# Two transformer blocks in one kernel: four layer seams run by token tile, x loaded in four transfers, the feed-forward of TensorE without its loop

## What is computed

```python
proj = x @ w_in[l]                      # 2048 -> 7168 columns
mix = concat(conv_mixer(...), hgrn2_mixer(...), retention_mixer(...))
x = layer_norm(ALPHA * x + mix @ w_out[l], ln1_g[l], ln1_b[l])
f = square(relu(x @ w_ff1[l]))          # 2048 -> 8192
x = layer_norm(ALPHA * x + f @ w_ff2[l], ln2_g[l], ln2_b[l])
```

## Time and profile before

| | |
|---|---|
| median of three runs | 3609.84 us |
| the profiled execution | 3611.74 us, its span 3609.9 us |
| mean granted TensorE clock | 0.981 |
| busy share of the span | TensorE 96%, VectorE 60%, ScalarE 45%, GpSimd 9% |
| chain that ended last | TensorE 85%, VectorE 8%, ScalarE 3%, DMA 2%, GpSimd 1%, issue 1% |
| moved by DMA | 617 MB, 171 GB/s over the span |

### The profile page before, as it was taken

One profiled execution on the slowest core, in us unless ns is written; L12 is line 12 of the kernel. 1 busy time (PEld: TensorE's weight loads), 2 busy tenths in 40 slices (PEclk: granted clock), 3 DMA queues, 4 the chain that ended last, 5 costly groups with the idle time before them and its releaser, 6 DMA issues.

```text
span 3609.9 us, 43760 instructions
## 1 busy us (share of the span) xinstructions
PE 3458.3 (96%) x16363; PEld 2890.7 (80%) x16363; DVE 2178.5 (60%) x2436; ACT 1618.2 (45%) x1953; POOL 329.4 (9%) x220
## 2 busy tenths in 40 slices
PE   7999999999999999999999999999999978999999
PEld 6888778888878787877888888888888777788877
DVE  5986565555555688865655555566456643656654
ACT  4544434444434346434444344444446533355553
POOL 0025000000000000330100000000000141000100
PEclk9999999999999999999999999999999989999999
DMA  6645555656555565446656565656656400565635
GB/s 211 189 139 158 180 182 186 192 186 187 186 185 185 171 194 156 146 146 204 220 189 187 192 187 191 188 185 206 184 173 178 143 6 14 185 191 174 177 121 163
DMA packets 311336, 617.02 MB, mean 171 GB/s; under 512 B 19305, under 2 KB 19305, under 8 KB 309243
## 3 DMA queue, kind: packets, MB, share of 16 engines
q1 hardware_dynamic: 306144, 591.73, 53.0%
q0 software_dynamic: 5024, 22.88, 1.9%
HBM read 612.44 MB, written 2.10 MB: 170 GB/s over the span
## 4 chain that ended last, share of the span: by engine, by line
PE 85%; DVE 8%; ACT 3%; DMA 2%; POOL 1%; issue 1%; SPq 0%; DVEq 0%; ACTq 0%; POOLq 0%
PE ps_unit L247 26%; PE ps_unit L249 26%; PE ps_unit L248 25%; DVE sb_w_lo L232 2%; PE ps_mix L2287 2%; DVE sb_conv_y L865 2%; PE ps_mix L939 1%; PE ps_mix L371 1%; PE ps_mix L525 1%; ACT sb_w_hi L225 1%; DMA sb_raw<-in_w_in_dram 1%; PE ps_mix L2285 0%; DMA sb_raw<-in_w_ff_dram 0%; DMA sb_raw<-in_e_w_in_dram 0%; PE ps_mix L2642 0%
## 5 line engine op out<-in xcount | busy, mean ns | idle before, releaser
L232 DVE TENSOR_TENSOR sb_w_lo<-sb_raw,sb_w_hi 128x1024 fp32r<-128x1024 f32 x1120 | 1407.6, 1269 | 1048.4 <-ACT sb_w_hi L225 1043.3
L225 ACT ACTIVATE sb_w_hi<-sb_raw 128x1024 fp32r<-128x1024 f32 x1120 | 1178.6, 1060 | 1483.4 <-DMA sb_raw<-in_w_ff_dram 740.9
L247 PE MATMUL ps_unit<-sb_w_hi,sb_a_hi 128*128 128x512 f32 x3456 | 1366.8, 395 | 26.7 <-DVE sb_a_lo L411 18.3
L249 PE MATMUL ps_unit<-sb_w_hi,sb_a_lo 128*128 128x512 f32 x3456 | 1351.7, 391 | 0.0
L248 PE MATMUL ps_unit<-sb_w_lo,sb_a_hi 128*128 128x512 f32 x3456 | 1351.3, 391 | 0.0
L247 PEld LDWEIGHTS ps_unit<-sb_w_hi,sb_a_hi 128*128 128x128 f32 x3456 | 653.6, 189 | 162.2 <-DVE sb_a_lo L411 19.8
L249 PEld LDWEIGHTS ps_unit<-sb_w_hi,sb_a_lo 128*128 128x128 f32 x3456 | 652.7, 189 | 138.2
L248 PEld LDWEIGHTS ps_unit<-sb_w_lo,sb_a_hi 128*128 128x128 f32 x3456 | 653.8, 189 | 132.3
L247 PE MATMUL ps_unit<-sb_w_hi,sb_f_hi 128*128 128x512 f32 x1024 | 400.0, 391 | 0.0
L249 PE MATMUL ps_unit<-sb_w_hi,sb_f_lo 128*128 128x512 f32 x1024 | 398.7, 389 | 0.0
L248 PE MATMUL ps_unit<-sb_w_lo,sb_f_hi 128*128 128x512 f32 x1024 | 398.4, 389 | 0.0
(11 more groups left out here) (447 smaller groups left out, 1986.1 us busy)
## 6 DMA issues: line engine op xcount, KB each, us to landing
sb_raw<-in_w_ff_dram SPq DMA_DIRECT2D x512, 512.0 KB, 3.7
sb_raw<-in_w_in_dram SPq DMA_DIRECT2D x224, 512.0 KB, 3.6
sb_raw<-in_e_w_in_dram SPq DMA_DIRECT2D x112, 512.0 KB, 3.5
sb_raw<-in_o_w_in_dram SPq DMA_DIRECT2D x112, 512.0 KB, 3.6
sb_raw<-in_w_out_dram SPq DMA_DIRECT2D x64, 512.0 KB, 4.5
sb_raw<-in_e_w_out_dram SPq DMA_DIRECT2D x32, 512.0 KB, 4.6
sb_raw<-in_o_w_out_dram SPq DMA_DIRECT2D x32, 512.0 KB, 3.8
sb_raw<-in_e_w_mem_kv_dram SPq DMA_DIRECT2D x16, 512.0 KB, 3.7
```

The lines of the kernel that those rows point to most:

```text
L225: k.nc.scalar.activation(k.w_hi[:, j], k.raw[:, j], ACT.Copy).then_inc(k.hi_ready, 1)
L232: k.nc.vector.tensor_tensor(k.w_lo[:, j], k.raw[:, j], k.w_hi[:, j].bitcast(F32), ALU.subtract).then_inc(k.lo_ready, 1)
L247: k.nc.tensor.matmul(acc, hi[:, kt, tokens], w_hi, start=kt == 0, stop=False)
L249: last = k.nc.tensor.matmul(acc, lo[:, kt, tokens], w_hi, start=False, stop=kt == KT - 1)
```

## The change

- At the four seams the last unit (`pe_seam_last`) runs blocks 0 to 3 for both tiles, then blocks 4 to 7 for tile 0, then blocks 4 to 7 for tile 1. The first unit behind the seam (`pe_seam_first`) runs blocks 0 to 3 for tile 0, then for tile 1, then 4 to 7 for both.
- A bank of a seam holds 512 channels of one tile (`SEAM_BANKS`). Residual, statistics and aggregate of tile 0 wait for `tile_done`, those of tile 1 for the unit. The norm is done for the first 1024 channels by tile, then for 512 channels of both tiles at a time, with the splits of blocks 3, 4 and 5 of the next unit between (`dve_seam`; `act_seam` on ScalarE).
- ALPHA is folded into the residual add of the out-projections; for the feed-forward GpSimd scales x behind the last bank of the seam (`pool_scale_residual`), and VectorE waits for that before its first residual there.
- At the start x comes in four transfers of 512 channels, each ahead of two blocks of weights, and splits and banks alternate on ScalarE and VectorE.
- On TensorE the groups of the feed-forward and the units of these out-projections are written out instead of looped.

The diff, cut:

```diff
+def sp_first_units(sp, k, x, weights):
+    w = weights.rearrange("(kt p) n -> p kt n", p=P)
+    for c in range(CONV_UNITS * BLOCKS):
+        j, at = c % BLOCKS, c // BLOCKS * NC
+        if c % 2 == 0 and c // 2 < D // NC:
+            cols = slice(c // 2 * NC, (c // 2 + 1) * NC)
+            sp.dma_start(k.x[:, :, cols], tokens(x)[:, :, cols]).then_inc(*k.x_in[c // 2].up(16))
+        sp.wait_ge(k.block_done, c + 1)
+        sp.dma_start(k.raw[:, j], w[:, KB * j:KB * (j + 1), at:at + NC]).then_inc(k.raw_ready[j], 16)
+    k.block0["sp"] += CONV_UNITS * BLOCKS
...
-def pe_block(pe, k, b0, c, hi, lo):
+def pe_block(pe, k, b0, c, hi, lo, tiles=range(TT)):
     s, j = c // BLOCKS % 2, c % BLOCKS
-    if j == 0:
-        pe.wait_ge(k.evacuated, b0 + (c + BLOCKS))
-    pe.wait_ge(k.lo_ready, b0 + (c + 1))
+    if 0 in tiles:
+        if j == 0:
+            pe.wait_ge(k.evacuated, b0 + (c + BLOCKS))
+        pe.wait_ge(k.lo_ready, b0 + (c + 1))
     for n in range(KB):
         kt = KB * j + n
-        for t in range(TT):
+        for t in tiles:
             tokens = slice(t * P, (t + 1) * P)
             acc = k.ps_unit[:, s, t, :]
             w_hi, w_lo = k.w_hi[:, j, n, :], k.w_lo[:, j, n, :]
             k.nc.tensor.matmul(acc, hi[:, kt, tokens], w_hi, start=kt == 0, stop=False)
             k.nc.tensor.matmul(acc, hi[:, kt, tokens], w_lo, start=False, stop=False)
             last = k.nc.tensor.matmul(acc, lo[:, kt, tokens], w_hi, start=False, stop=kt == KT - 1)
-    last.then_inc(k.block_done, 1)
+    if TT - 1 in tiles:
+        last.then_inc(k.block_done, 1)
+    return last
...
+SEAM = BLOCKS // 2
+SEAM_BANKS = ((0, 0), (0, 1), (1, 0), (1, 1), (0, 2), (1, 2), (0, 3), (1, 3))
...
+def pe_seam_bank(pe, k, tile, n):
+    t, c = SEAM_BANKS[n]
+    pe.wait_ge(*k.turn_source.next("pe"))
+    if n >= 4:
+        pe.wait_ge(*k.turn_lo.next("pe bank"))
+    for x in range(4):
+        last = k.nc.tensor.transpose(k.ps[:, n % 4, x * P:(x + 1) * P], tile(4 * c + x, t), k.ident)
+    last.then_inc(*k.turned.up())
+def pe_seam_last(pe, k, b0, u, hi, lo, tile):
+    c0 = u * BLOCKS
+    for j in range(SEAM):
+        pe_block(pe, k, b0, c0 + j, hi, lo)
+    for j in range(SEAM, BLOCKS):
+        last = pe_block(pe, k, b0, c0 + j, hi, lo, (0,))
+    last.then_inc(*k.tile_done.up())
+    for j in range(SEAM, BLOCKS):
+        pe_block(pe, k, b0, c0 + j, hi, lo, (1,))
+        if j == BLOCKS - 2:
+            pe_seam_bank(pe, k, tile, 0)
+    pe_seam_bank(pe, k, tile, 1)
+def pe_seam_first(pe, k, b0, tile):
+    for t in range(TT):
+        for j in range(SEAM):
+            if j % 2 == 0:
+                pe.wait_ge(*k.turn_lo.next("pe"))
+            pe_block(pe, k, b0, j, k.a_hi, k.a_lo, (t,))
+            if (t, j) in ((0, 2), (0, 3), (1, 1), (1, 2)):
+                pe_seam_bank(pe, k, tile, {(0, 2): 2, (0, 3): 3, (1, 1): 4, (1, 2): 5}[t, j])
+    for j in range(SEAM, BLOCKS):
+        if j % 2 == 0:
+            pe.wait_ge(*k.turn_lo.next("pe", TT))
+        pe_block(pe, k, b0, j, k.a_hi, k.a_lo)
+        if j == SEAM:
+            for n in (6, 7):
+                pe_seam_bank(pe, k, tile, n)
+    k.turn_lo.next("pe bank", 4)
...
+def act_seam(act, k, b0, c0, root):
+    act_sqrt_table(k)
+    act_split(act, k, b0, c0 + SEAM - 1)
+    for t in range(TT):
+        root(t)
+        for n in (2 * t, 2 * t + 1):
+            act_seam_bank(act, k, n)
+    for c in (SEAM, SEAM + 1):
+        act_split(act, k, b0, c0 + c)
+    for n in range(4, 8):
+        act_seam_bank(act, k, n)
...
+def dve_seam(dve, k, b0, u, chunk, norm):
+    c0 = (u + 1) * BLOCKS
+    def statistics(t):
+        cols = slice(chunk * NC, (chunk + 1) * NC)
+        x = k.x[:, t, cols]
+        if t == 0:
+            dve.wait_ge(*k.tile_done.next("dve"))
+        else:
+            wait_unit(dve, k, b0, u)
+        ins = add_residual(k, x, k.ps_unit[:, u % 2, t], norm.scale)
+        if t == 0:
+            ins.then_inc(*k.dve_step.up())
+            dve.wait_ge(*k.dve_step.now())
+        else:
+            ins.then_inc(k.evacuated, BLOCKS)
+            dve.wait_ge(k.evacuated, b0 + (u + 3) * BLOCKS)
+        ins = k.nc.vector.bn_stats(k.stats[:, t, chunk, :], x)
+        if t == 0:
+            ins.then_inc(*k.dve_step.up())
+            dve.wait_ge(k.stats_ready, k.stats_units - 1)
+            dve.wait_ge(*k.dve_step.now())
+        else:
+            ins.then_inc(k.stats_ready, 1)
+            dve.wait_ge(k.stats_ready, k.stats_units)
+        norm.aggregate(dve, k, t)
+    statistics(0)
+    norm.columns(dve, k, 0, (0, 1))
+    dve_seam_bank(dve, k, 0)
+    statistics(1)
+    dve_seam_bank(dve, k, 1)
+    dve_split(dve, k, b0, c0 + SEAM - 1)
+    norm.columns(dve, k, 1, (0, 1))
+    dve_seam_bank(dve, k, 2)
+    dve_seam_bank(dve, k, 3)
+    for c in (2, 3):
+        norm.columns(dve, k, None, (c,))
+        dve_split(dve, k, b0, c0 + SEAM + c - 2)
+        for t in range(TT):
+            dve_seam_bank(dve, k, 2 * c + t)
+class LayerNorm:
+    def __init__(self, scale):
+        self.scale = scale
+    def aggregate(self, dve, k, t):
+        k.nc.vector.bn_aggr(k.mv[:, t, :], k.stats[:, t].rearrange("p c s -> p (c s)")).then_inc(*k.aggregated.up())
+    def columns(self, dve, k, tile, chunks):
+        v = k.nc.vector
+        tiles = range(TT) if tile is None else (tile,)
+        if tile == 0:
+            dve.wait_ge(*k.row_in.next("dve", 32))
+        dve.wait_ge(*k.aggregated.now())
+        parts = [(t, slice(c * NC, (c + 1) * NC)) for c in chunks for t in tiles]
+        for t, cols in parts:
+            last = v.scalar_tensor_tensor(k.x[:, t, cols], k.x[:, t, cols], k.mv[:, t, 0:1], k.gain[:, cols],
+                                          ALU.subtract, ALU.mult)
+        last.then_inc(*k.dve_step.up())
+        if tile is not None:
+            dve.wait_ge(*k.root.next("dve"))
...
+class RootMeanSquare:
...
+        v = k.nc.vector
+        tiles = range(TT) if tile is None else (tile,)
+        if tile is not None:
+            if tile == 0:
+                dve.wait_ge(*k.row_in.next("dve", 16))
+            dve.wait_ge(*k.rms_root.next("dve"))
+            v.reciprocal(k.ss[:, tile, 1:2], k.ss[:, tile, 1:2]).then_inc(*k.dve_step.up())
+            dve.wait_ge(*k.dve_step.now())
+        for c in chunks:
+            cols = slice(c * NC, (c + 1) * NC)
+            for t in tiles:
+                v.scalar_tensor_tensor(k.normed_x[:, t, cols], k.x[:, t, cols], k.ss[:, t, 1:2], k.gain[:, cols],
+                                       ALU.mult, ALU.mult).then_inc(*k.turn_source.up())
...
+def dve_out_units(dve, k, norm):
+    first = k.block0["dve"]
+    k.block0["dve"] += OUT_UNITS * BLOCKS
+    k.stats_units += OUT_UNITS
+    for u in range(OUT_UNITS - 1):
+        for c in range(AHEAD, AHEAD + BLOCKS):
+            if c == AHEAD + BLOCKS - 1:
+                residual(dve, k, first, u, u, norm.scale)
+            dve_split(dve, k, first, u * BLOCKS + c)
+    last = OUT_UNITS - 1
+    for c in range(AHEAD, BLOCKS + SEAM - 1):
+        dve_split(dve, k, first, last * BLOCKS + c)
+    dve_seam(dve, k, first, last, last, norm)
 def pe_units(pe, k, units, tile=None):
...
+def residual(dve, k, b0, u, chunk, scale=None):
     wait_unit(dve, k, b0, u)
     cols = bass.ds(chunk * NC, NC)
-    k.nc.vector.tensor_tensor(k.x[:, :, cols], k.x[:, :, cols], k.ps_unit[:, u % 2],
-                              ALU.add).then_inc(k.evacuated, BLOCKS)
+    add_residual(k, k.x[:, :, cols], k.ps_unit[:, u % 2], scale).then_inc(k.evacuated, BLOCKS)
...
-def dve_scale_residual(dve, k):
-    dve.wait_ge(*k.turn_lo.now())
-    k.nc.vector.tensor_scalar(k.x[:], k.x[:], ALPHA, None, ALU.mult).then_inc(*k.dve_step.up())
-    dve.wait_ge(*k.dve_step.now())
...
+def pool_scale_residual(pool, k):
+    k.nc.gpsimd.tensor_scalar(k.x[:], k.x[:], ALPHA, None, ALU.mult).then_inc(*k.x_scaled.up())
...
+                pe_seam_first(pe, k, b0, tile)
+                continue
+            if after and g0 == FF_GROUPS - 1 and u == FF_UNITS - 1:
+                pe_seam_last(pe, k, b0, u, hi, lo, after)
+                continue
             for j in range(BLOCKS):
                 if u == 4 and j == 0:
...
-    def turn_step(u, j):
-        if u == 0:
-            pe_turn_step(pe, k, tile, j)
-    pe_turn_start(pe, k, tile)
-    group(0, 0, turn_step)
-    with pe.Fori(0, FF_GROUPS - (2 if between else 1)) as q:
-        group(q, 1)
-    if between:
-        group(0, FF_GROUPS - 1, between)
+    group(0, 0)
+    for q in range(1, FF_GROUPS):
+        group(0, q, between if q == FF_GROUPS - 1 else None)
 def turned_unit(k, u):
     return k.ps[:, 2 * (u % 2):2 * (u % 2) + 2, :].rearrange("p b (a s) -> p (b a) s", a=2)
...
+            if norm and u == FF_UNITS - 1:
+                dve_split(dve, k, b0, u * BLOCKS + AHEAD + 4)
+                dve_seam(dve, k, b0, u, u - 4, norm)
+                continue
             for j in range(AHEAD + 4, AHEAD + 8):
```

(49 more changed lines are left out.)

117 lines of the change are left out of this document (87 added, 30 removed).

## The result

The kernel after the change takes **3580.3 us** (median of six runs, 3578.3 to 3581.6), beside 3616.7 us (3609.0 to 3619.8, six runs) of the kernel before on the same chip. The ratio is **0.9908**, 95% interval 0.9898 to 0.9919: faster by 0.9%. Forecast were 3563.6 us and a range of 3552 to 3580, so the change is faster, as forecast, but by 0.92% where 1.28% were forecast, and the time lies just above the range. (The six executions before spread over 11 us, so the quotient of the two medians, 0.9899, is not quite the ratio.) The profiled execution took 3581.3 us for a span of 3579.5: 30.4 us less span than before, where the sum had 46.2.

A forecast was written before the change was run, and what follows sets the result against it. TensorE, busy 96% of the span, was taken as the bound. Seams 12.4, 8.1 and 7.4, start 10.0, loop 6.6 and ReLU 1.7 sum to 46.2 us saved, giving 3563.6 us against the median; range 3552 to 3580.

The forecast's parts named there:

- the part on ALPHA: Two seams before a feed-forward: GpSimd's scale takes 3.7 us (or 7.6), costing TensorE 2.0 us more in each.
- rival (1): GpSimd's scale runs at the product's rate, 7.6 us; split 3.9 later, clock drops: time 3574, chance 0.10.
- The mechanism of the hold: Seams before a feed-forward: VectorE's split of block 6 is held until GpSimd's scale ends; TensorE waits 2.0 us.
- The walk of the seam: Step-by-step count of a norm seam after the change: waits 4.8 plus eight banks 2.8, 7.6 us instead of 15.9.
- Seam 2: Seam into layer 1, without a scale: cost falls from 15.7 to 7.6 us, a gain of 8.1.
- The start: Kernel start, x in quarters: first matmul at 14.3 instead of 24.27 us, -10.0 us, bounds 8 and 11.5.
- The loop: Layer 0's feed-forward back edges: unlooped code loses the waits on "issue" and low clock, -6.6 us, bounds 4.7 and 7.2.
- the ReLU: Layer 1's squared ReLU: TensorE's single 1.7 us wait disappears, -1.7 us, bounds 0 and 1.9.
- (2): Low clock enters the seams: three norm seams lose 1.5 to 3 us each, time 3568 to 3573, chance 0.14.
- (3): VectorE needs 0.1 to 0.2 us more at each of 25 seam steps, 3 us per seam: 3575, chance 0.06.
- (4): Straight code stalls for fetches like the loop and x's quarters arrive no earlier: time 3577, chance 0.05.
- (5): Slower: TensorE stays at the low clock through each seam, time about 3690, chance 0.02.

The follow-up runs named there:

- e5: Changed kernel with GpSimd's scale replaced by a copy of x onto itself, ALPHA left out of that residual: 3573.3 us, one run.
- e1: Changed kernel without GpSimd's scale, ALPHA folded into the residual adds of the first feed-forward group: 3560.4 us, ratio 0.9855.
- e9: e1 with five GpSimd instructions (scales, a copy, a product) on an unused tile ahead of everything: 3563.8 us, one run.
- e11: e1 with GpSimd's first seven small transfers waiting for the second quarter of x: 3558.4 us, ratio 0.9852.
- e6: Changed kernel with GpSimd's scale replaced by the product x * x of the same 4096 elements: 3572.8 us, one run.
- e2: Changed kernel with the scale on VectorE again, one pass behind the last bank: 3569.7 us, ratio 0.9888.
- e7: Kernel before with the new start alone (x in four transfers, splits and banks in turn): 3603.7 us, ratio 0.9978.

## Why the prediction was wrong, and where it was right

**The step that failed** is one term of the part on ALPHA: "I take 3.7, since scale and copy both read one tensor". The number of inputs does not set GpSimd's time. Measured for 4096 elements: copy 3.61, product 7.01, scale 10.56 us. The choice between the two bounds of the earlier trace rows was argued by likeness, and both bounds were taken for ends although neither row is a scale. The upper one was 3 us too low.

**A second term of the same step** was put at nothing: the clock behind the hold. The forecast charges 2.0 us for the wait and no low clock, and rival (1) prices the clock only for a wait of nearly 6. With e5's copy, which takes the forecast's 3.7 us, the wait is the forecast's 2.0, and 1.5 us of low clock come on top in each seam: -5.1 and -4.9 where -6.2 was forecast. So with the right length too the two seams would have given some 2.4 us less than the sum has.

**The range** ended 0.3 us short of the time. Its upper end also rests on a slip: two of the rivals together, at the prices that the text gives (10.4, up to 9, and 12), come to 3583 to 3586, not 3580. The bounds named for its lower end come to 3553.5, not 3552.

**The mechanism of the hold was right.** A split behind the scale is held, it is the split of block 6, and TensorE waits for it: forecast 2.0, measured 7.1. The forecast's rule (the held split ends 1.1 us behind GpSimd) would with 10.56 us have given 8.9. Behind the wait come 2.4 us of low clock. 7.3 and 2.4, less 2.0, are 7.7; the table has 7.4, and most of the difference is that the rest of the seam costs 7.4 and not 7.6.

**The walk of the seam held in its sum, and partly by luck.** Forecast 7.6 us instead of 15.9. With the scale away (e1) the seam is 8.5 cheaper, 7.4. Read by pitches, as the forecast did, the waits of e1's first seam come to 3.6 us where 4.8 were forecast, the longest 1.4 where mine was 2.2 (the list of waits has 1.2, since it leaves out what the pipeline takes to refill). A bank of four transposes costs 0.45 us and not 0.35, since the pitch behind it is 0.09 longer: 3.6 for eight where 2.8 were put. The two errors nearly cancel. Seam 2 gave 8.2 for 8.1 and the last 7.0 for 7.4.

**The start**: 9.9 for 10.0, but in another way. The first matmul is at 15.12 and not at 14.3; another 0.8 comes back before the first seam, in units that had waits of their own before. That 9.9 meets 10.0 is luck: ten profiles with this start (without e9 and e11) have gained 9.8 to 13.1 us by the first seam.

**The loop**: 7.1 for 6.6. Layer 0's three later groups took 178.32, 180.27 and 181.70 us; the first two take 177.72 each now, and the third does too but for the first bank of the seam, which lies in it. The gain stands at the two back edges, 2.8 us at 863 and 4.3 at 1044. The Trainium skill (Runtime: NRT & Kernel Launch, Instruction fetch mechanics) says that a taken branch out of the prefetched code stalls for a fetch, and these two agree. The further 3 us that the rule would have given in layer 1 did not come: behind the seam nothing was gained there but the 1.9 us of the ReLU.

**The rivals.** (1) had the right place and the right sign; at the product's rate it gave 3574, and e6, which is that case, took 3572.8 in its one run. The truth lay beyond it. (2) did not happen among the waits that it named: between 482 and 504 us of after, short matmul runs, transposes and waits of up to 1.2 us together, the granted clock is 1.00:

```profile
482.00:504.00 22.00, 19.99 (x100) 15.61 (x99) 18.62 (x28) 7.58 (x12) 1.89 (x1) 1.00 0.54 168
```

But the low clock did enter the two seams with a scale, behind the wait for the held split. It fell behind the stops of 7 us in after, 5.3 in e6 and 1.9 in e5, in both seams each. Behind e2's stops of 2.4 us it fell in one seam and not in the other. What decides it there is not shown. (3) is refuted by e1, (4) by the list of waits and by e7, (5) by the clock.
